# Attention steps placed between the q, k and v layers of a two-block transformer kernel, with the low parts of these layers' weights on VectorE

## The chip, the cores and the metric

The kernel runs on one core of a Trainium2 chip. The metric is device time in microseconds (us), the median of the timed runs. TensorE (PE) multiplies, VectorE (DVE) and ScalarE (ACT) work element by element, GpSimd (POOL) does too, SyncE (SP) starts transfers. Every engine works through a queue of its own in order and meets the others at semaphores.

## What is computed

Two transformer blocks in a row on 256 tokens of width 1024, float32. The first is a mixer (gated delta rule and an S5 state-space layer), a cross attention `xa` (4 heads of 256) and a gated feed-forward layer. The second has two layers: stick-breaking and MoBA attention with rotary positions (`ab`), then forgetting attention (`fox`), each followed by a memory cross attention (`xa0`, `xa1`, 4 heads of 64) and a feed-forward layer with a short convolution. Cut to what the change touches:

```python
def sb_moba_mixer(h, positions, w_in, w_out):
    qkv = h @ w_in                                   # q, k, v: 16 heads of 64
    o_sb = stick_breaking_attention(q[:, :8], k[:, :8], v[:, :8])
    o_moba = moba_attention(rope(q[:, 8:], positions), rope(k[:, 8:], positions), v[:, 8:])
    return merge_heads(jnp.concatenate([o_sb, o_moba], axis=1)) @ w_out
def fox_mixer(h, w_in, b_f, w_out):
    q, k, v, f_logit = ...                           # from h @ w_in; 16 heads of 64
    log_f = jax.nn.log_sigmoid(f_logit + b_f)
    return merge_heads(forgetting_attention(q, k, v, log_f)) @ w_out
# stick breaking, per head: z = q k^T / 8
#   log_1mb = where(past, log_sigmoid(z) - z, 0); tail = reverse cumsum(log_1mb) - log_1mb
#   a = where(past, exp(log_sigmoid(z) + tail), 0); o = a v
# forgetting, per head: p = softmax(q k^T / 8 + c[t] - c[s], causal); c = cumsum(log_f)
```

With 256 tokens a MoBA block holds them all, so that attention is a plain causal softmax.

## The kernel before

Activations lie feature-major: 8 tiles of 128 features x 256 tokens. All weights come in one list of slots of 128 x 1024 float32 (512 KB), transferred in turn into six `w_raw` buffers. From `x_v` on a slot is split: ACT writes the high part `w_hi` (line 857), DVE (line 1303) or POOL (line 1945) the rest `w_lo`, each into one of three buffers. `lo_on_pool` says which: outside the feed-forward layers every third slot is POOL's. `three` (line 351) then makes each product of three fp32r products: high x high, low input, low weight. `ahead(s)` stands in the ACT and DVE queues and makes the parts up to slot s+2; a high part waits until PE has left the slot three before.

A feature-major layer (`fm`) takes one slot of 8 blocks for one output tile, 24 products of 256 columns. A token-major one (`tok_slot`, the v layers) takes two input tiles per slot, 12 products of 512 columns. Accumulators are banks 0 and 1 in turn; a product waits until the one two before is read out. Reading out multiplies with `R`, the reciprocal root mean square (`scaled`, line 1438), which is computed while the first products of a layer run. Its sums are `mean_square` (line 423), f32 products; a f32 product is two passes in the trace. In front of `ab` two such norms follow each other (`fin1`, `mx0`).

The order is written out by hand on each engine: all of `ab_q`, `ab_k` (with `rope` products, line 778, in between), `ab_v`, then the attention head by head, then `ab_o`; `fox` alike. In `attention` a head's scores (line 684; for fox selector products 690 and 692 and the mask 694) go to one bank, DVE takes the maximum (1671, 1672 or 1674), ACT the exponentials (1163), DVE divides (1680, 1683), PE turns the probabilities (707), ACT copies them (1173 to 1176), PE multiplies with v (`values`, 727), ACT and DVE split the result (1186, 1697). Three heads are in flight. Stick breaking has scores (803, 804), three ACT steps, two DVE steps (1820, 1822), cumulative sums as products (814 to 816), and a DVE step (1813). A head has 64 features, so its products use half of PE's rows (scores) or columns (values). During these attentions the slots of the next layer wait, as all buffers are full.

Of the kernel before, what the change touches and what calls it, by code (L numbers as in the profile page):

```python
# [8 lines left out]

# [7 lines left out]
P = 128  # L17
T = 256
D = 1024
KD = D // P  # L20
# [6 lines left out]
NF = 22  # L27
# [16 lines left out]
FIRST, _n = {}, 0  # L44
for _name, _kind, _k, _m in LINEARS:
    FIRST[_name] = _n
    _n += 3 * NF if _kind == "ffn" else _k * _m // 8
SLOTS = _n
SHAPE = {name: (k, m) for name, _, k, m in LINEARS}
# [19 lines left out]
MEM_SUMS_AT = {6 + m: m for m in range(KD)}  # L69

# [98 lines left out]
def lo_on_pool(s):  # L169
# [3 lines left out]
    for name in ("ffn0", "ffn1", "ffn2"):  # L173
        if FIRST[name] <= s < FIRST[name] + 3 * NF:
            return (s - FIRST[name]) % 3 == 2
    return s % 3 == 0


def build(nc, io, known):
    with ExitStack() as ctx:  # L180
# [53 lines left out]
        def scores_bank(h):  # L234

            return bank[(2, 3, 0, 1)[h % 4]]

        def tok_bank(name, nh, tt):


            if nh and name != "x_v":
                return bank[6 + tt]
            return bank[(ACC_OF[name] + 2 * nh + tt) % 2]
# [35 lines left out]
        PROB = area(6144, 2, 2, T)  # L279
        PROBT = area(7168, 2, 2, T)  # L280
        SBA, SBM = area(8192, 3, 384), area(9344, 2, 384)
# [15 lines left out]
        def _(sp):  # L297
            sp.dma_start(PARS[:], io["pars"]).then_inc(*inc("pars_landed", "pars", by=16))
            sp.dma_start(H[:], io["x"]).then_inc(*inc("x_landed", "x", by=16))
            for s in range(SLOTS):  # L300
# [16 lines left out]
                sp.dma_start(RAW[:, s % RAW_SLOTS, :], io_w[s]).then_inc(  # L317
# [9 lines left out]
        def _(pe):  # L327
            mm, tp = nc.tensor.matmul, nc.tensor.transpose
            acc = [0]

            def acc_take(n=1):

                t0 = acc[0]
                acc[0] += n
                for t in range(t0, t0 + n):
                    if t >= 2:
                        pe.wait_ge(*at(("acc", t - 2)))
                return t0
# [25 lines left out]
            def fm(name, m, x, x_ready, sums=None, whole_sum=None):  # L364
# [3 lines left out]
                t = acc_take()  # L368
                out = bank[t % 2][:, 0:T]
                order = [(k + 4) % 8 for k in range(8)] if name == "w_out" else range(K)  # L370
                for n, k in enumerate(order):
                    b = m * K + k
                    s = FIRST[name] + b // 8
# [16 lines left out]
            def tok_slot(name, j, x, x_ready):  # L390
# [3 lines left out]
                s = FIRST[name] + j  # L394
                slot_ready(s)
                for b in range(8 * j // w, 8 * (j + 1) // w):
                    nh, k = b // K, b % K
                    if k == 0 and (nh == 0 or name == "x_v"):
                        acc_take(2)
                    if nh == 0:  # L400
                        pe.wait_ge(*at(x_ready(k)))
                    for tt in range(TT):
                        out = tok_bank(name, nh, tt)[:, 0:w * P]
# [10 lines left out]

            def tok(name, x, x_ready):
                for j in range(SHAPE[name][0] * SHAPE[name][1] // 8):
                    tok_slot(name, j, x, x_ready)
# [159 lines left out]
            for s, (name, j) in enumerate(STEPS):  # L577
# [8 lines left out]
                if s == 0:  # L586
                    pe.wait_ge(*at("cons"))
                    fm(name, j, x, lambda k: ("whole", ready, k), lambda k: mean_square("x", k))
# [1561 lines left out]
```

## Time and profile before

| | |
|---|---|
| timed runs, us | 1395.13, 1417.39, 1421.9 (median 1417.39) |
| profiled execution, us | 1396.11, of which 1394.3 is the span that the profile shows |
| mean granted PE clock | 0.953 |
| busy, us | PE 1301.1, DVE 843.1, ACT 685.9, POOL 257.7 |
| transferred | 187.90 MB, 135 GB/s over the span |

Times in the profile count from the start of the span. The profiled execution is one run; stage and step times of it add up to its own 1396.11 us and not to the median. PE, DVE and ACT overlap, so their sums exceed the span.

### The profile page before, as it was taken

What the parts mean: (1) busy time and instruction counts of PE and PEld (TensorE: products, weight loads), DVE (VectorE), ACT (ScalarE), POOL (GpSimd) and SP (SyncE); (2) the same over time, 40 slices, a digit from 0 to 9 for tenths busy, and PEclk for the clock granted to TensorE, in tenths of its full rate; (3) what the DMA queues carried; (4) which work ended last, traced back from release to release, by engine and by line L of the source; (5) the groups of instructions that cost most, each with busy time, mean ns of one, the idle gap of its engine ahead of it and who ended that gap; (6) DMA issues with size and microseconds to landing.
All of it is one profiled execution on the core that took longest, in us unless ns stands there. A gap on an engine that the chain in (4) does not pass through costs nothing.

```text
span 1394.3 us, 22964 instructions
## 1 busy us (share of the span) xinstructions
PE 1301.1 (93%) x9136; PEld 1180.3 (85%) x9136; DVE 843.1 (60%) x1511; ACT 685.9 (49%) x1197; POOL 257.7 (18%) x160
## 2 busy tenths in 40 slices
PE   6999899899999999898899799999999996999997
PEld 5777689798999999797648599999997584999996
DVE  2899676564654444565435567777644465677775
ACT  3352525454544444634435455555634455655554
POOL 5000000121222222222002022222222010222221
PEclk9999999989999999999659799999999999999999
DMA  7233322233455555344003145555454032355551
GB/s 308 91 106 108 120 91 91 76 122 121 139 190 185 185 183 184 111 160 166 0 1 125 57 139 188 185 185 183 155 184 161 1 107 76 135 184 181 182 182 46
DMA packets 51225, 187.90 MB, mean 135 GB/s; under 512 B 5680, under 2 KB 5808, under 8 KB 50736
## 3 DMA queue, kind: packets, MB, share of 16 engines
q1 hardware_dynamic: 51120, 186.44, 38.8%
q8 instruction: 73, 1.20, 0.3%
q14 instruction: 32, 0.26, 0.1%
HBM read 185.37 MB, written 1.05 MB: 134 GB/s over the span
## 4 chain that ended last, share of the span: by engine, by line
PE 79%; DVE 8%; ACT 7%; issue 4%; POOL 2%; DMA 0%; DVEq 0%; ACTq 0%; POOLq 0%
PE banks L351 58%; PE banks L727 4%; PE banks L381 4%; PE banks L684 3%; ACT w_hi L857 2%; PE banks L707 2%; PE banks L423 1%; DVE w_lo L1303 1%; PE banks L406 1%; PE banks L545 1%; DVE h L1653 1%; ACT arena L1163 1%; PE banks L474 1%; PE banks L555 1%; DVE a_lo L1315 1%
## 5 line engine op out<-in xcount | busy, mean ns | idle before, releaser
L1945 POOL TENSOR_TENSOR w_lo<-w_raw,w_hi 128x1024 fp32r<-128x1024 f32 x99 | 238.7, 2411 | 1110.4 <-ACT w_hi L857 1110.4
L857 ACT ACTIVATE w_hi<-w_raw 128x1024 fp32r<-128x1024 f32 x313 | 329.0, 1052 | 197.2 <-PE banks L351 190.5
L351 PE MATMUL banks<-a_hi,w_hi 128*128 128x256 f32 x1432 | 413.9, 289 | 7.4 <-DVE arena L1438 4.9
L351 PE MATMUL banks<-a_lo,w_hi 128*128 128x256 f32 x1432 | 407.5, 285 | 0.0
L351 PE MATMUL banks<-a_hi,w_lo 128*128 128x256 f32 x1432 | 407.3, 284 | 0.0
L1303 DVE TENSOR_TENSOR w_lo<-w_raw,w_hi 128x1024 fp32r<-128x1024 f32 x214 | 263.4, 1231 | 90.8 <-ACT w_hi L857 90.7
L351 PEld LDWEIGHTS banks<-a_hi,w_hi 128*128 128x128 f32 x1432 | 277.0, 193 | 10.1 <-DVE arena L1438 5.1
L351 PEld LDWEIGHTS banks<-a_lo,w_hi 128*128 128x128 f32 x1432 | 277.1, 193 | 0.6
L351 PEld LDWEIGHTS banks<-a_hi,w_lo 128*128 128x128 f32 x1432 | 276.8, 193 | 0.0
L351 PE MATMUL banks<-b_hi,w_hi 128*128 128x256 f32 x880 | 257.1, 292 | 18.4 <-DVE h L1653 6.4
L351 PE MATMUL banks<-b_lo,w_hi 128*128 128x256 f32 x880 | 253.3, 288 | 0.0
L351 PE MATMUL banks<-b_hi,w_lo 128*128 128x256 f32 x880 | 253.1, 288 | 0.0
L351 PEld LDWEIGHTS banks<-b_hi,w_hi 128*128 128x128 f32 x880 | 173.1, 197 | 24.5 <-issue 13.8
L351 PEld LDWEIGHTS banks<-b_lo,w_hi 128*128 128x128 f32 x880 | 173.5, 197 | 0.0
L351 PEld LDWEIGHTS banks<-b_hi,w_lo 128*128 128x128 f32 x880 | 173.2, 197 | 0.0
L1206 ACT ACTIVATE arena<-arena,pars 128x256 f32<-128x256 f32 x88 | 53.0, 602 | 131.5 <-DVE arena L1726 131.5
L1726 DVE TENSOR_TENSOR arena<-banks,rstd 128x256 f32<-128x256 f32 x132 | 55.8, 424 | 101.3 <-PE banks L351 93.0
L1732 DVE SCALAR_TENSOR_TENSOR arena<-arena,pars 128x255 f32<-128x255 f32 x88 | 59.8, 680 | 60.7 <-ACT arena L1206 60.7
L381 PE MATMUL banks<-early,w_raw 128*128 128x256 f32 x400 | 94.2, 390 | 0.2 <-ACT v_mem L951 0.2
L381 PEld LDWEIGHTS banks<-early,w_raw 128*128 128x128 f32 x400 | 77.5, 196 | 14.7 <-issue 3.1
L882 ACT ACTIVATE a_hi<-h,pars 128x256 fp32r<-128x256 f32 x64 | 32.4, 506 | 62.4 <-DVE h L1653 60.2
L1163 ACT ACTIVATE arena<-banks,small 128x128 f32<-128x128 f32 (+1 forms) x72 | 30.9, 435 | 61.9 <-PE banks L707 45.3
(324 smaller groups left out, 1531.0 us busy)
## 6 DMA issues: line engine op xcount, KB each, us to landing
w_raw<-in_weights SPq DMA_DIRECT2D x342, 512.0 KB, 3.5
h<-in_x SPq DMA_DIRECT2D x1, 1024.0 KB, 4.9
arena<-in_mem SPq DMA_DIRECT2D x1, 1024.0 KB, 13.2
early<-in_mem SPq DMA_DIRECT2D x1, 1024.0 KB, 14.9
out_h<-h SPq DMA_DIRECT2D x2, 512.0 KB, 2.7
cons<-in_cons SPq DMA_DIRECT2D x1, 962.0 KB, 7.7
arena<-in_late SPq DMA_DIRECT2D x1, 448.0 KB, 4.3
pars<-in_pars SPq DMA_DIRECT2D x1, 290.5 KB, 2.9
```

The lines of the kernel that those rows point to most:

```text
L351: ins = mm(out, l, r, start=start and n == 0, stop=stop and n == 2, skip_group_check=check)
L381: ins = mm(out, raw(s, b % 8), x[:, k, :], start=n == 0, stop=n == K - 1)
L684: ins = mm(out, q[rows, tile, tt * P:(tt + 1) * P], k[rows, tile, 0:keys], start=n == 0, stop=n == len(parts) - 1 and not causal and not bias)
L727: ins = mm(out, v[:, kt, c:c + min(dims, P)], probs(h, kt)[:, lo_t:T], start=kt == 0, stop=kt == TT - 1)
L857: do(WHI[:, n % SPLIT_SLOTS, :], RAW[:, n % RAW_SLOTS, :], ACT.Copy).then_inc(*inc("w_hi_made", ("w_hi", n)))
L882: do(x[0][:, m, :], src, ACT.Copy, scale=par(g, m)).then_inc(*inc("input_hi", ("a_hi", tag, m)))
L1163: do(PROB[:, h % 2, tt, 0:keys], scores_bank(h)[:, tt * T:tt * T + keys], ACT.Exp, bias=SMALL[:, o + tt:o + tt + 1], accum_out=SMALL[:, o ...
L1206: do(FC[:, 2 * (f % 2) + g, :], FS[:, 2 * (f % 3) + g, :], ACT.Identity, scale=par(f"cw{conv}", 88 + g * NF + f), bias=par(f"cb{conv}", g ...
L1303: v.tensor_tensor(WLO[:, n % SPLIT_SLOTS, :], RAW[:, n % RAW_SLOTS, :], WHI[:, n % SPLIT_SLOTS, :].bitcast(F32), ALU.subtract).then_inc(*i ...
L1726: v.tensor_tensor(x, acc_bank(t), R[:], ALU.mult).then_inc(*inc("ffn_scaled", ("fs", tag, f, g), ("acc", t)))
L1732: step(v.scalar_tensor_tensor(c[:, 1:T], x[:, 0:T - 1], par(f"cw{conv}", 44 + g * NF + f), c[:, 1:T], ALU.mult, ALU.add), label="ffn_conv")
L1945: g.tensor_tensor(WLO[:, n % SPLIT_SLOTS, :], RAW[:, n % RAW_SLOTS, :], WHI[:, n % SPLIT_SLOTS, :].bitcast(F32), ALU.subtract).then_inc(*i ...
```

## The change

The slots of `ab` and `fox` come in another order: four v slots (half of v), for fox the gate's slot, then 20 units u: q 0, k 0, q 1, k 1, ... q 7, k 7 and the other four v slots. All sixteen heads are treated as eight pairs p, two heads in the two halves of a 128-row tile. Tables such as `SB_SCORES_AT` say after which unit PE issues which step of which pair; DVE and ACT follow one and two units later. A pair's products alternate between its two heads and go to two banks (scores) or to two halves of one (values); DVE and ACT steps take both heads at once. Both masks of a head become one product. The values of pairs 4 to 7 are issued after the first four products of `ab_o` (`fox_o`). `xa` is woven into `x_q` in the same way, head by head. `xa0` and `xa1` stay whole, but issue all scores first. The cosine and sine steps (`rope_args`, `rope_angles`) move into `ffn0`. `lo_on_pool` is false for all slots of the `ab` and `fox` q, k, v and gate layers. The first accumulators of a stage lie in banks 0, 1, 6 and 7. The last quarter of v is read out by DVE.

```diff
+def unit(b, u):
+
+    return (f"{b}_{'qk'[u % 2]}", u // 2) if u < 16 else (f"{b}_v", u - 12)
+
+
+def in_turn():
+    for name, kind, k, m in LINEARS:
+        if name in ("ab_q", "fox_q"):
+            b = name[:-2]
+            yield from ((f"{b}_v", j) for j in range(4))
+            if b == "fox":
+                yield "fox_f", 0
+            yield from (unit(b, u) for u in range(20))
+        elif name[:3] in ("ab_", "fox") and name[-2:] != "_o":
+            continue
+        else:
+            yield from ((name, j) for j in range(3 * NF if kind == "ffn" else k * m // 8))
+
+
+SLOT = {x: s for s, x in enumerate(in_turn())}
+ROW_OF = [ROW[name] + j for name, j in SLOT]
...
+SB_SCORES_AT = {2 * p + 2: p for p in range(4)}
+SB_CUM_AT = {2 * p + 4: p for p in range(4)}
+SB_VALUES_AT = {2 * p + 5: p for p in range(4)}
+ROPE_Q_AT = {2 * p + 1: p for p in range(4, 8)}
+ROPE_K_AT = {2 * p + 2: p for p in range(4, 8)}
+MOBA_SCORES_AT = {2 * p + 3: p for p in range(4, 8)}
+MOBA_TURN_AT = {2 * p + 5: p for p in range(4, 8)}
+FOX_SCORES_AT = {2 * p + 2: p for p in range(8)}
+FOX_TURN_AT = {2 * p + 4: p for p in range(8)}
+FOX_VALUES_AT = {2 * p + 5: p for p in range(4)}
+NEXT_V = {"mx0": "ab_v", "mx1": "fox_v"}
+X_SCORES_AT = {2: 0, 4: 1, 6: 2}
+X_TURN_AT = {4: 0, 6: 1}
+X_VALUES_AT = {5: 0, 7: 1}
...
+    for name in ("ab", "fox"):
+        if FIRST[f"{name}_v"] <= s < FIRST[f"{name}_o"]:
+            return False
...
+            for u in range(KD):
+                fm("x_q", u, A, lambda k: ("a_lo", "xa", k), whole_sum="xa")
+                if u in X_SCORES_AT:
+                    x_scores(X_SCORES_AT[u])
+                if u in X_TURN_AT:
+                    x_turn(X_TURN_AT[u])
+                if u in X_VALUES_AT:
+                    x_values(X_VALUES_AT[u])
+            x_scores(3)
+            x_turn(2)
+            x_values(2)
+            x_turn(3)
+            residual("x_o", B, lambda k: ("att_in", "xa", k), ahead_of={6: lambda: x_values(3)})
...
+            def pair_values(block_, p, ready, probs):
+
+                pe.wait_ge(*at(ready))
+                if p >= 4:
+                    for tt in range(TT):
+                        pe.wait_ge(*at((f"{block_}_v", "out", 1, tt)))
+                else:
+                    pe.wait_ge(*at((f"{block_}_v", "out", 0, 1)))
+                if p == 0:
+                    pe.wait_ge(*at(("acc", LAST_IN_6[block_])))
+                elif p <= 4:
+                    pe.wait_ge(*at(("o_free", block_, p - 1)))
+                else:
+                    pe.wait_ge(*at(("pt", "fox" if block_ == "fox" else "moba", 6 if p < 7 else 7)))
+                o = values_bank(p)
+                for kt in range(TT):
+                    for e in range(2):
+                        ins = mm(o[HALF[e], kt * P:T], VF[:, kt, (2 * p + e) * 64:(2 * p + e) * 64 + 64],
+                                 probs[:, e, 0:T] if kt == 0 else probs[:, e, T:384], start=kt == 0, stop=kt == 1)
+                ins.then_inc(*inc("values_done", ("o", block_, p)))
...
+            def mask(b):
+
+                blocks_0_2 = bank[b].rearrange("p (a b) -> p a b", a=4)[:, 0:3:2, :]
+                return mm(blocks_0_2, BFC[:, 0, :], BFC[:, 1, :].unsqueeze(1).to_broadcast([P, 2, P]),
+                          start=False, stop=True, skip_group_check=True)
+
+            def pair_scores(p):
+
+                for tt in range(TT):
+                    for e, b in enumerate(pair_banks(p)):
+                        mm(bank[b][:, tt * P:tt * P + (tt + 1) * P], QF[HALF[e], p, tt * P:(tt + 1) * P],
+                           KF[HALF[e], p, 0:(tt + 1) * P], start=tt == 0, stop=False, skip_group_check=True)
...
+            for j in range(4):
+                tok_slot("ab_v", j, A, lambda k: ("a_lo", "mx0", k), sums_mx0)
+            for u in range(20):
+                name, m = unit("ab", u)
+                if u < 16:
+                    fm(name, m, A, lambda k: ("a_lo", "mx0", k))
+                else:
+                    tok_slot(name, m, A, lambda k: ("a_lo", "mx0", k))
+                if u == 1:
+                    rstd_cols("mx0", R)
+                if u in ROPE_Q_AT:
+                    rope("ab_q", ROPE_Q_AT[u])
+                if u in ROPE_K_AT:
+                    rope("ab_k", ROPE_K_AT[u])
+                if u in SB_SCORES_AT:
+                    sb_scores(SB_SCORES_AT[u])
+                if u in MOBA_SCORES_AT:
+                    moba_scores(MOBA_SCORES_AT[u])
+                if u in SB_CUM_AT:
+                    sb_cum(SB_CUM_AT[u])
+                if u in MOBA_TURN_AT:
+                    pair_turn("moba", MOBA_TURN_AT[u])
+                if u in SB_VALUES_AT:
+                    p = SB_VALUES_AT[u]
+                    pair_values("ab", p, ("sb_a", p), SBA[p % 2])
...
+            def memory_attention(l):
+
+                tag = f"xa{l}"
+                for p in range(2):
+                    pe.wait_ge(*at((f"m_q{l}", "scaled", p)))
+                    pe.wait_ge(*at((f"m_k{l}", "scaled", p)))
+                    for tt in range(TT):
+                        for e, b in enumerate(pair_banks(p)):
+                            ins = mm(bank[b][:, tt * T:(tt + 1) * T], QF[HALF[e], p, tt * P:(tt + 1) * P],
+                                     KM[HALF[e], l, p, :], start=tt == 0, stop=True, skip_group_check=True)
+                            if tt == 1:
+                                ins.then_inc(*inc("scores_done", ("s", tag, 2 * p + e)))
+                for h in range(4):
+                    pe.wait_ge(*at(("p", tag, h)))
+                    for tt in range(TT):
+                        for kt in range(TT):
+                            ins = tp(bank[2 + h][:, kt * T + tt * P:kt * T + tt * P + P],
+                                     MPROB[h // 2][:, h % 2, tt, kt * P:(kt + 1) * P], ident)
+                    ins.then_inc(*inc("turned_done", ("tp", tag, h)))
+                    if h >= 2:
+                        memory_values(l, h - 2)
+                for h in range(2, 4):
+                    memory_values(l, h)
...
+            for u in range(1, 20):
+                if u <= 16:
+                    q_or_k("ab", u - 1)
+                if u == 1:
+                    dve.wait_ge(*at("late"))
+                if u == 2:
+                    cols("mx0", 0)
+                if u - 1 in ROPE_Q_AT:
+                    rope("ab_q", ROPE_Q_AT[u - 1])
+                if u - 1 in ROPE_K_AT:
+                    rope("ab_k", ROPE_K_AT[u - 1])
+                if u - 1 in SB_CUM_AT:
+                    sb_arg(SB_CUM_AT[u - 1])
+                if u - 2 in SB_SCORES_AT:
+                    sb_keep_past(SB_SCORES_AT[u - 2])
+                if u - 2 in MOBA_SCORES_AT:
+                    pair_norm("moba", MOBA_SCORES_AT[u - 2])
+                if u - 1 in MOBA_SCORES_AT:
+                    pair_max("moba", MOBA_SCORES_AT[u - 1])
+                ahead(SLOT[unit("ab", u)])
+                if u - 1 in SB_VALUES_AT:
+                    pair_lo("ab", SB_VALUES_AT[u - 1])
```

How this moves the instructions shows at two places. The first is PE in stage ab. Before, the moba heads stand behind all layers; the rows are one head and a piece of the next (707 turns, 684 scores, 694 mask, 727 values):

```order
3190 L684 MATMUL banks<-arena 128x128
3191 L694 MATMUL banks<-bf_consts 128x128
3192 L684 MATMUL banks<-arena 128x256
3193 L694 MATMUL banks<-bf_consts 128x128
3194 L727 MATMUL banks<-arena 64x256
3195 L727 MATMUL banks<-arena 64x128
3196 L707 MATMUL banks<-cons,arena 128x128 x3
3197 L684 MATMUL banks<-arena 128x128
3198 L694 MATMUL banks<-bf_consts 128x128
```

After, unit 11 (`ab_k` 5): the last product of its slot (line 398), then the rope product of q 5 (879), scores of pair 4 (840), masks (833), values of pair 3 (826), then the next slot:

```order
3010 L398 MATMUL banks<-a_hi,w_lo 128x256
3011 L879 MATMUL banks<-arena 128x256
3012 L840 MATMUL banks<-arena 128x128 x2
3013 L840 MATMUL banks<-arena 128x256 x2
3014 L833 MATMUL banks<-bf_consts 128x2x128 x2
3015 L826 MATMUL banks<-arena 64x256 x2
3016 L826 MATMUL banks<-arena 64x128 x2
3017 L398 MATMUL banks<-a_hi,w_hi 128x256
```

The same products now stand between two slots, in twos, and the turns come two units later.

The second is DVE in stage ab. Before, around k 5 of `ab_k` (1438 reads out a tile, 1789 to 1791 are rope, 1303 a low part):

```order
494 L1438 SCALAR_TENSOR_TENSOR arena<-banks,rstd 128x256
495 L1789 TENSOR_TENSOR arena<-banks,arena 128x256
496 L1790 TENSOR_TENSOR arena<-arena 128x256
497 L1791 TENSOR_TENSOR arena<-arena 128x256
498 L1438 SCALAR_TENSOR_TENSOR arena<-banks,rstd 128x256
499 L1789 TENSOR_TENSOR arena<-banks,arena 128x256
500 L1790 TENSOR_TENSOR arena<-arena 128x256
501 L1791 TENSOR_TENSOR arena<-arena 128x256
502 L1303 TENSOR_TENSOR w_lo<-w_raw,w_hi 128x1024
```

After, unit 13 and the start of unit 14 (1678 reads out, 2092 to 2094 rope, 1952 and 1955 divide, 1546 a low part, 1944 and 1945 maxima):

```order
547 L1678 SCALAR_TENSOR_TENSOR arena<-banks,rstd 128x256
548 L2092 TENSOR_TENSOR arena<-banks,arena 128x256
549 L2093 TENSOR_TENSOR arena<-arena 128x256
550 L2094 TENSOR_TENSOR arena<-arena 128x256
551 L1952 RECIPROCAL small<-small 128x4
552 L1955 TENSOR_TENSOR arena<-arena,small 128x2x128
553 L1955 TENSOR_TENSOR arena<-arena,small 128x2x256
554 L1546 TENSOR_TENSOR w_lo<-w_raw,w_hi 128x1024
555 L1678 SCALAR_TENSOR_TENSOR arena<-banks,rstd 128x256
556 L2092 TENSOR_TENSOR arena<-banks,arena 128x256
557 L2093 TENSOR_TENSOR arena<-arena 128x256
558 L2094 TENSOR_TENSOR arena<-arena 128x256
```

Every unit now has its low part on DVE, and the attention's steps stand in front of it.

## Rows read from the trace of the kernel before

**Rows 1.** The page, part 1: TensorE's busy time, share, instructions.
```profile
PE 1301.1 (93%) x9136; PEld 1180.3 (85%) x9136; DVE 843.1 (60%) x1511; ACT 685.9 (49%) x1197; POOL 257.7 (18%) x160
```

**Rows 2.** Table by stage (start:end, us, busy of PE, PEld, DVE, ACT, POOL; clock; DMA).
```profile
332.00:352.00 20.00, 16.80 (x82) 13.83 (x83) 7.69 (x19) 7.74 (x24) 0.00 (x0) 1.00 0.09 28
...
658.00:734.00 76.00, 65.60 (x217) 40.53 (x217) 25.57 (x71) 32.82 (x90) 0.45 (x1) 0.61 0.02 8
767.00:788.00 21.00, 14.88 (x50) 8.03 (x51) 6.54 (x19) 7.13 (x24) 0.00 (x0) 0.67 0.11 41
996.00:1073.00 77.00, 75.34 (x526) 70.27 (x525) 37.86 (x61) 36.48 (x49) 19.29 (x8) 1.00 0.49 168
1073.00:1125.00 52.00, 48.16 (x275) 28.39 (x276) 22.39 (x87) 26.13 (x107) 0.00 (x0) 1.00 0.05 17
```

**Rows 3.** Chain that ended last: start us, us, what.
```profile
389.39 175.90 PE banks L351 x1464
...
569.28 0.58 PE banks L351 x3
...
579.10 1.28 ACT L862
...
586.96 26.02 PE banks L351 x192
...
649.37 7.53 PE banks L351 x33
...
734.05 9.97 PE banks L351 x72
...
1124.63 5.96 PE banks L351 x48
```

**Rows 4.** Timeline of PE, one head of the fox attention (start, us).
```profile
1081.13 0.86 PE L727 MATMUL banks<-arena 128*64 128x256 f32 x4
1081.92 0.55 PE L707 MATMUL banks<-cons,arena 128*128 128x128 f32 x3
1082.40 0.49 PE L684 MATMUL banks<-arena 64*128 64x128 f32 x2
...
1083.09 0.70 PE L684 MATMUL banks<-arena 64*128 64x256 f32 x2
1083.72 0.28 PE L690 MATMUL banks<-fox_selector,arena 96*128 96x256 bf16 x1
...
1084.10 0.65 PE L727 MATMUL banks<-arena 128*64 128x256 f32 x2
```

**Rows 5.** The chain in the S5 stage: full passes, row groups, column groups.
```profile
107.34 7.11 PE banks L381 x32
114.45 1.06 PE banks L459 x8
...
119.16 1.85 PE banks L474 x16
```

**Rows 6.** Groups by line and shape, DVE, 634 to 734 us (busy, mean ns).
```profile
L1303 DVE TENSOR_TENSOR w_lo<-w_raw,w_hi 128x1024 fp32r<-128x1024 f32 x5 | 6.1, 1222 | 1.4 <-ACT w_hi L857 1.4
...
L1820 DVE SCALAR_TENSOR_TENSOR arena<-banks,arena 128x384 f32<-128x384 f32 x8 | 4.4, 552 | 6.1 <-ACT arena L1262 6.1
...
L1789 DVE TENSOR_TENSOR arena<-banks,arena 128x256 f32<-128x256 f32 x4 | 1.7, 425 | 3.9 <-PE banks L778 3.1 <-DVE h L1804 0.7
L1680 DVE RECIPROCAL small<-small 128x2 f32<-128x2 f32 x8 | 1.2, 156 | 2.0 <-ACT arena L1163 2.0
```

**Rows 7.** Timelines of DVE and of POOL, 647 to 651 us.
```profile
647.60 2.62 DVE L1804 SCALAR_TENSOR_TENSOR h<-h,pars,mem_rstd 128x256 f32<-128x256 f32 x1
...
647.50 2.44 POOL L1945 TENSOR_TENSOR w_lo<-w_raw,w_hi 128x1024 fp32r<-128x1024 f32 x1 [7.24 <-ACT w_hi L857]
```

**Rows 8.** Timeline of PE, memory attention xa1, and what follows it.
```profile
1157.09 1.99 PE L684 MATMUL banks<-k_mem,arena 64*128 64x256 f32 x12 [0.69 <-DVE arena L1438]
...
1173.61 0.39 PE L351 MATMUL banks<-b_hi,w_hi 128*128 128x256 f32 x1
```

More of the change, by code:

```diff
@@ L10 @@
+import itertools
 from contextlib import ExitStack
@@ new lines, in rope @@
+            def rope(name, p):
+                pe.wait_ge(*at((name, "scaled", p)))
+                if name == "ab_q" and p == 4:
+                    pe.wait_ge(*at("late"))
+                    pe.wait_ge(*at(("acc", LAST_IN_7["ab"])))
+                else:
+                    pe.wait_ge(*at(("rope_read", *(("ab_q", p) if name == "ab_k" else ("ab_k", p - 1)))))
+                mm(bank[7][:, 0:T], rot_m, (QF if name == "ab_q" else KF)[:, p, :], start=True,
+                   stop=True).then_inc(*inc("rope_done", ("rope", name, p)))
@@ L1266, in _ @@
+            tok_out("ab_v", 1, VF, 0, (0,))
+            pair_turned("moba", 7)
+            for p in range(4, 8):
+                pair_hi("ab", p)
             residual("ab_o", "xa0", "g2_xa0")
             plain("m_q0")
-            attention("xa0", 4, 64, False)
+            memory_attention("xa0")
             residual("m_o0", "f1", "g2_ffn0")
             ffn("ffn1", "f1", "mx1", "g2_mix1", conv=0)
-            plain("fox_q")
-            plain("fox_k")
-            plain("fox_f")
-            for s in range(2):
-                ahead(FIRST["fox_v"] + s)
+            ahead(SLOT["fox_f", 0])
@@ L1277, in _ @@
+            ahead(SLOT[unit("fox", 0)])
             act.wait_ge(*at("fox_x"))
@@ L1826, in _, with rope @@
-            attention("moba", 8, 64, True, 4)
+            dve.wait_ge(*at("mx0_second"))
+            step(v.tensor_tensor(R, MR1, MR2, ALU.mult), ("r", "mx0"))
+            ahead(SLOT[unit("ab", 0)])
+            def rope(name, p):
+                x = (QF if name == "ab_q" else KF)[:, p, :]
+                dve.wait_ge(*at(("rope", name, p)))
+                if name == "ab_q" and p == 4:
+                    dve.wait_ge(*at("cos"))
+                else:
+                    dve.wait_ge(*at(("roped", *(("ab_q", p) if name == "ab_k" else ("ab_k", p - 1)))))
+                step(v.tensor_tensor(POSF, bank[7][:, 0:T], SIN, ALU.mult), ("rope_read", name, p), label="rope_vec")
+                step(v.tensor_tensor(x, x, COS, ALU.mult), label="rope_vec")
+                v.tensor_tensor(x, x, POSF, ALU.add).then_inc(*inc("rope_vec", ("roped", name, p)))
@@ L1827, in _ @@
+            v_out("ab")
+            for p in range(4, 8):
+                pair_lo("ab", p)
             residual("ab_o", "xa0", "g2_xa0")
             plain("m_q0", QF, "xa0", 0.125)
[L1829 removed]
+            memory_attention("xa0")
             residual("m_o0", "f1", "g2_ffn0")
             ffn("ffn1", "f1", "mx1", "g2_mix1", conv=0)
[L1832 to L1834 removed]
+            ahead(SLOT["fox_v", 3])
@@ L1841, in _ @@
+            ahead(SLOT[unit("fox", 0)])
+            q_or_k("fox", 0)
+            ahead(SLOT[unit("fox", 1)])
             dve.wait_ge(*at("fox_ln"))
```

831 lines of the change are left out of this document (458 added, 373 removed).

## The prediction

> **What bounds the kernel now.** I read the page first, then the table by stage, then the chain of waits. TensorE (PE) is busy 93% of the span [rows 1], so time can only go where PE runs slowly or does work that can be had for less. The table by stage [rows 2] shows where that is. From 658 to 734 us (the stick-breaking and moba attentions) PE is busy 65.6 of 76 us, but its granted clock is 0.61 and the DMA queues move 8 GB/s: PE waits, computes at half clock and no weight moves. The fox attention (1073 to 1125) runs at full clock, PE busy 48.2 of 52. In the layers in front of it (996 to 1073) PE is busy 75.3 of 77 us while VectorE (DVE) works 37.9 and ScalarE (ACT) 36.5: both are half idle there and have room for attention work. The chain [rows 3] gives the unit prices: a slot of a feature-major layer (24 products) costs 175.90/1464 x 24 = 2.88 us of PE, a slot of a token-major one (12 products with 512 columns) 7.53/33 x 12 = 2.74 us.
>
> **Stage ab, PE's work at full clock.** The new order begins with the first four slots of `ab_v`. Each of its eight input tiles costs six products of 0.228 us and two mean-square sums, f32, two passes of 0.22 us each: 2.25 us, so 18.0 us. PE starts them when the old kernel starts `ab_q` (569.3) [rows 3]. In the old kernel PE stands until 587.0, because the accumulator of `ab_q` 0 can only be emptied once `R` exists. Now `ab_v` fills banks 0 and 1 without `R`, and q 0 and k 0 have banks of their own, so 5.8 us of products cover the chain that makes `R` (I estimate 4 to 5 us from the last sum: eight steps on ACT and DVE of the 0.43 us kind of [rows 6], and a table load of 1.28 [rows 3]). The rest: 16 q and k slots, 46.1 us; four more v slots, 11.0; eight rope products of 0.44, 3.5.
>
> The attention itself goes by pairs of heads, and a pair's products alternate between halves of the array. The trace of before has such alternation elsewhere [rows 5]: a full f32 pass of 256 columns takes 7.11/32 = 0.222 us; eight passes that alternate between row groups take 1.06 us, 0.133 each; sixteen that alternate between column groups take 1.85 us, 0.116 each. The memory attention's first three heads, which happen to follow each other in opposite halves, need 1.99 us for 12 passes, 0.166 each [rows 8]. I take the first two. Scores of a pair (four passes with 256 columns, four with 128): 4 x 0.133 + 4 x 0.067 = 0.80 us. Values: 0.46 + 0.23 = 0.70. Without overlap either is 1.33. The single head of now pays more [rows 4]: its 256-column score product stands 0.63 us before the next starts, its values 0.79, its three turns 0.48, the whole head 2.97 from one values step to the next. A stick-breaking pair: 0.80 + cumulative products 2 x 512 columns at full size, 1.78, + 0.70 = 3.3; four are 13.1. A moba pair: 0.80 + two masks 0.25 + turns 0.96 + 0.70 = 2.7; four are 10.8. For the entry into each of 28 inserted pieces I add 0.15 us, the surplus of a half-array product over the full one (0.63 against 0.44) [rows 4, 5], rounded down: 4.2. Sum 18.0 + 46.1 + 11.0 + 3.5 + 13.1 + 10.8 + 4.2 = 106.7. `ab_o` would begin at 569.3 + 106.7 = 676.0 instead of 734.1 [rows 3], with the values of pairs 4 to 7 counted though they now lie behind its first four products. **58 us less.** Half of that is the clock: the 76 us at 0.61 are 46 at full clock. The rest is pairing, waits of PE and the covered `R`.
>
> TensorEngine Tiling (Array Packing) of the Trainium skill, section Theoretical Speedup, allows up to 2x where a dimension is 64 or less; by it scores and values of a pair would cost 0.67 each instead of 0.80 and 0.70, 2.6 us less over 16 pairs. The same page, Key Properties, says that a change of tiling mode drains the engine, which speaks against products of other shapes woven in; the trace agrees in that the lone product above costs 0.63.
>
> **Who else must keep up in ab.** PE reaches unit u+2 two units after DVE may begin its low part, so a late DVE queue stops PE. DVE rows [rows 6]: low part 1.22, scaled output and each rope step 0.43, 384 columns 0.55 (768: 0.95), reciprocal 0.16. Heaviest are units 9 to 17, where rope, moba and the end of stick-breaking meet. DVE has there 9 low parts 11.0, 8 scaled 3.4, 8 ropes 10.3, four 768-column steps 3.8, three maxima (0.42 + 0.69) 3.3, three normalisations (0.16 + 0.42 + 0.69) 3.8, two low parts of values 0.8: 36.4 us. PE has eight q/k and v units, rope, three and a half moba pairs and two values, in all 40 us. So DVE is 90% full and PE stays the bound. Eight of the stage's 24 low parts were POOL's. Taking them from POOL costs DVE 9.8 us, hidden as just counted, and gives some back: in 647.6 a step with two SBUF inputs took 2.62 us instead of under 0.5, as long as POOL's own low part ran [rows 7]. The GPSIMD Engine Reference of the Trainium skill, section Specifications, says that the two share their SBUF interface when a DVE instruction has two SBUF inputs; the trace agrees, 2.62 us.
>
> ACT has per two units 2 x 1.06 of high parts and four exponentials, some 6 us against 9. `ahead` for a later slot stands in front of the attention steps in its queue and waits only for a slot that PE has left. The cosine and sine steps move into `ffn0`, where DVE has half its time free and PE is 5.8 us behind the prepared slots: 2.6 us hidden. Weights: a slot's transfer needs 3.1 us at the 168 GB/s of the layers [rows 2] and units now last 3.3 to 5.4 us, so transfers are easier than before.
>
> **Stage fox.** From 996: 8 x (1.37 + 0.44) = 14.5; `fox_f` 2.9; q, k 46.1; v 11.0; eight pairs of 0.80 + selector and mask products 1.0 (0.38 and 0.27 per head, less half of the masks) [rows 4] + 0.96 + 0.70 = 3.46, 27.7; 20 pieces x 0.15 = 3.0. Sum 105.2, `fox_o` at 1101.2 instead of 1124.6 [rows 3]: **23 us less**. A two-unit period is 9.3 us for PE and about 6 for DVE.
>
> **Memory attentions xa0, xa1.** Now some 20 us (at clock 0.67) and 16.5 us from the first scores to the first product of `m_o` [rows 2, 8]. With all scores issued first, DVE carries it: 1.1 us to the first head's scores, four maxima of 0.69, four normalisations of 0.85, then turn 0.6, copy 0.6, values 0.6, high and low 0.8: 9.7 to the second tile, about 9.6 to the first product. **10 and 7 us less.** Stage xa (332 to 352) has full-size products that cannot be paired; PE is busy 16.8 of 20 us [rows 2], and scores, turn and values of its last head are still exposed. I take 2 us, with bounds 0 and 3.
>
> **Sum.** 58 + 23 + 17 + 2 = 100 us. The profiled execution took 1396.1 us (span 1394.3), so it would be 1296. The three timed runs were 1395, 1417 and 1422: the median lies 21 above the profiled one. Part of that may be half-clock time that goes with this stage; I add some 9 and forecast **1305 us**. A measurement of this kernel can hardly tell less than 2% (28 us) from no change.
>
> **Rivals.**
> *Halves do not overlap in this place* (other banks, weight loads of 64 rows between passes). For it: the three heads above reach only 0.166 [rows 8]. Against it: both alternations in rows 5. Price 16 pairs x (0.53 + 0.63) = 19 us: 1324.
> *DVE's queue becomes the bound.* In-order waits (cumulative sum, logarithm, maximum) stand in front of each low part; 90% leaves little, and 768-column broadcasts have no row. If each of 36 woven units ends 0.7 us late, 25 us: 1330. The weave would then do only part of what it says, since PE would stand at the weights instead of at the scores.
> *The clock falls in the woven stage* as it did from 672 on, after PE had stood for scores. At 0.61 the 107 us of ab would last 68 longer: 1373. Against it: the fox attention with the same kinds of products held 1.00 [rows 2].
> *Slower:* each inserted piece waits for its answer from ACT and DVE, unhidden, with the layers' products stopped behind it. A round trip per head is 16.5/4 = 4.1 us [rows 8]; 55 pieces would cost 226 against the 100 saved. It decides from 1.8 us per piece on; at 4.1 the kernel takes 1530. Against it: one to two units (2.9 to 5.8 us) lie between a piece and its answer.
>
> **How the numbers follow.** Forecast 0.58, no overlap 0.12, DVE 0.16, clock 0.07, slower 0.04, other 0.03. The range runs from 1280 (pairs at 0.67, no entry cost, median as the fastest runs) to 1345 (both middle rivals together, or one of them with the 21 us); clock and slower are left out. Faster by over 2%: the first three and part of the clock case, 0.89. Within 2%: rest of clock and other, 0.07. Slower: 0.04.
>
> **What would show it.** Right: `ab_o` some 107 us after `ab_v`'s first product; granted clock 1.0 in between; a pair's eight score passes in 0.8 us; fox stage 105 us; memory attentions under 10.5. Wrong: PE waiting for `w_lo` from DVE for more than 5 us in all, or for probabilities; score pairs of 1.3 us; clock under 0.9 in the woven stages; transfers of weights landing late.

## Result and profile after

The changed kernel takes 1316.33 us (median of 1313.02, 1316.21, 1316.45 and 1318.37), the kernel before 1406.26 in the runs beside it (1394.44 to 1421.9): a ratio of 0.9435, interval 0.9402 to 0.9469. The forecast was 1305, range 1280 to 1345. The runs of before fall into two groups, near 1395 and near 1419; those of after do not, and the ratio compares with the lower group. The profiled execution took 1313.02 us with a span of 1311.2, so 83.1 us of span were saved where 100 were forecast.

The page of after, part 1, answers to [rows 1]:

```profile
PE 1226.5 (94%) x9112; PEld 1140.2 (87%) x9112; DVE 849.1 (65%) x1445; ACT 668.4 (51%) x1136; POOL 219.7 (17%) x144
```

PE is busy 74.6 us less with nearly the same number of instructions: fewer of them run at half clock, and heads no longer run singly. The mean clock is 0.984 instead of 0.953.

The table by stage of after, with the columns of [rows 2]: passage into `ab_v`, woven ab, `ab_o`, xa0, passage into `fox_v`, the rest of fox.

```profile
562.70:598.00 35.30, 23.88 (x82) 18.51 (x83) 9.80 (x17) 14.25 (x26) 0.00 (x0) 0.85 0.17 56
598.00:681.30 83.30, 83.30 (x628) 74.55 (x628) 64.52 (x109) 48.31 (x83) 2.12 (x1) 1.00 0.39 127
681.30:717.60 36.30, 34.20 (x283) 31.93 (x281) 23.25 (x38) 20.42 (x34) 8.01 (x4) 1.00 0.44 142
717.60:728.20 10.60, 8.08 (x41) 4.54 (x41) 6.02 (x13) 6.66 (x22) 0.00 (x0) 0.84 0.18 63
936.20:958.90 22.70, 17.00 (x68) 13.14 (x67) 9.88 (x16) 10.23 (x17) 0.00 (x0) 0.92 0.33 113
958.90:1045.00 86.10, 84.50 (x684) 75.97 (x684) 52.65 (x95) 46.48 (x105) 2.38 (x1) 1.00 0.37 122
```

The second row is the change at work: 83.3 us without one moment in which PE stands, at full clock, with weights at 127 GB/s. The stage of before that had clock 0.61 and 8 GB/s [rows 2] is gone. The first and the fifth row are new: while PE works on the first four v slots it is busy 23.9 of 35.3 us and 17.0 of 22.7, and the clock sinks.

Stage by stage, from first product to first product in both chains, where the time went:

| part | before | after | saved | forecast |
|---|---|---|---|---|
| start to `x_q` | 311.2 | 306.9 | 4.2 | 0 |
| `x_q` to ffn0 | 78.2 | 75.8 | 2.4 | 2 |
| ab's first product to `ab_o` | 164.8 | 118.6 | | |
| `ab_o` to xa0 | 33.6 | 36.3 | 43.5 for both | 58 |
| xa0's scores to `m_o` | 19.9 | 10.6 | 9.4 | 10 |
| fox's first product to `fox_o` | 128.3 | 108.8 | | |
| `fox_o` to xa1 | 32.5 | 35.2 | 16.8 for both | 23 |
| xa1's scores to `m_o` | 16.5 | 10.3 | 6.2 | 7 |

The 2.7 us more in the `_o` layers are the values of four pairs that the change put there. The 4.2 us at the start are no work of the change: there the two traces differ in granted clock only (0.83 in before's 40 to 60 us, 1.00 in after's). That part of the kernel is the same in every experiment below, and its clock changes from run to run: 0.83 in the profiled runs of experiments 4 and 6, 0.91 in those of experiments 1 and 2, 1.00 in that of experiment 5. So these 4.2 us are chance.

The chain of after between 566 and 582 us shows the new stand, that is, the time in which PE waits with work left to do:

```profile
566.56 0.45 PE banks L470 x2
...
567.10 0.39 ACT squares L1044
...
567.94 1.05 ACT w_hi L1029
...
569.01 0.04 DVE w_lo L1546
569.05 1.11 issue
570.16 0.42 DVE h L2052
...
570.61 0.49 DVE a_lo L1558
...
571.24 2.31 PE banks L398 x6
573.54 1.71 PE banks L470 x4
```

Read it as a ring. PE forms the sums of tile 1 (L470); that frees the buffer for the squares of tile 2; behind them in ACT's queue stands the high part of the next v slot; DVE's low part waits for it, and behind that low part stand `h` of tile 3 and `a_lo` of tile 2, on which PE waits. PE stands 3.81 us, and what follows runs at half clock: four sums in 1.71 instead of 0.86 us. The same comes again at 577 and 587. In front of fox the ring closes three times too, with stands of 1.90 us; behind the first two PE goes on at full clock, and only behind the third (953.4) does half clock follow.

The woven part in the chain of after, for [rows 4]:

```profile
607.02 0.63 PE banks L852 x4
607.66 0.22 PE banks L855 x4
...
648.33 0.86 PE banks L840 x8
649.19 0.33 PE banks L833 x2
649.51 0.80 PE banks L826 x8
650.32 3.06 PE banks L398 x24
...
653.81 2.87 PE banks L398 x24
...
658.29 0.66 PE banks L806 x6
```

Scores of a pair take 0.86 us (0.85 in stick breaking), masks 0.33, values 0.80, the turns 0.66, and the slot behind values 3.06 instead of 2.87.

The chain in xa1, for [rows 8]:

```profile
1080.16 1.11 PE banks L935 x8
...
1083.25 0.69 DVE arena L1921
...
1088.45 1.89 PE banks L957 x12
```

`m_o` begins at 1090.48, 10.3 us after the first scores, and VectorE's maxima and divisions fill the middle of it, as counted.

### The profile page after: what moved, and what is told of

It reads as the page before. It is cut to its first block, busy times and chain, and to the rows that moved or that the text cites. A ratio compares the mean times of both kernels' runs of the same rounds, so it can differ in the third digit from the quotient of the medians.

```text
span 1311.2 us, 22739 instructions
## 1 busy us (share of the span) xinstructions
PE 1226.5 (94%) x9112; PEld 1140.2 (87%) x9112; DVE 849.1 (65%) x1445; ACT 668.4 (51%) x1136; POOL 219.7 (17%) x144
## 4 chain that ended last, share of the span: by engine, by line
PE 81%; DVE 9%; ACT 5%; issue 4%; DMA 1%; POOL 1%; SPq 0%; DVEq 0%; ACTq 0%
PE banks L398 62%; PE banks L429 5%; ACT w_hi L1029 2%; PE banks L470 2%; DVE w_lo L1546 1%; PE banks L455 1%; PE banks L592 1%; PE banks L826 1%; DVE h L1889 1%; DVE a_lo L1558 1%; PE banks L521 1%; PE banks L602 1%; PE banks L840 1%; ACT squares L1044 1%; PE banks L608 1%
## 5 line engine op out<-in xcount | busy, mean ns | idle before, releaser
L2279 POOL TENSOR_TENSOR w_lo<-w_raw,w_hi 128x1024 fp32r<-128x1024 f32 x83 | 200.7, 2418 | 1065.5 <-ACT w_hi L1029 1065.5
L1546 DVE TENSOR_TENSOR w_lo<-w_raw,w_hi 128x1024 fp32r<-128x1024 f32 x230 | 283.6, 1233 | 101.1 <-ACT w_hi L1029 100.8
L398 PE MATMUL banks<-b_hi,w_hi 128*128 128x256 f32 x880 | 254.3, 289 | 21.7 <-DVE h L1889 7.1
L398 PEld LDWEIGHTS banks<-b_hi,w_hi 128*128 128x128 f32 x880 | 170.4, 194 | 28.2 <-issue 14.9
L398 PEld LDWEIGHTS banks<-b_lo,w_hi 128*128 128x128 f32 x880 | 170.7, 194 | 0.0
L1054 ACT ACTIVATE a_hi<-h,pars 128x256 fp32r<-128x256 f32 x64 | 32.5, 507 | 70.4 <-DVE h L1889 57.2
L470 PE MATMUL banks<-squares,cons 128*128 128x256 f32 x112 | 35.6, 434 | 13.5 <-DMA cons<-in_cons 9.9
```

Source lines behind the costliest of these rows:

```text
L398: ins = mm(out, l, r, start=start and n == 0, stop=stop and n == 2, skip_group_check=check)
L470: ins = mm(bank[2][:, 0:T] if out is None else out, con("ones_d", P), SQ[:, sq_slot(tag, m), :], start=m == 0 and tag != "mem1", stop=m == ...
L1054: do(x[0][:, m, :], src, ACT.Copy, scale=par(g, m)).then_inc(*inc("input_hi", ("a_hi", tag, m)))
L1546: v.tensor_tensor(WLO[:, n % SPLIT_SLOTS, :], RAW[:, n % RAW_SLOTS, :], WHI[:, n % SPLIT_SLOTS, :].bitcast(F32), ALU.subtract).then_inc(*i ...
L2279: g.tensor_tensor(WLO[:, n % SPLIT_SLOTS, :], RAW[:, n % RAW_SLOTS, :], WHI[:, n % SPLIT_SLOTS, :].bitcast(F32), ALU.subtract).then_inc(*i ...
```

## Experiments

The times are medians of the timed runs; where a stage is named it is read from the profile of that kernel.

**1. The high part in front of the squares.**

```diff
                         hi_gained(tag_next, m, A, H[:, m, :], g_next, ("h", tag_next, m))
+                    if tag_next in NEXT_V and m in (1, 3, 5):
+                        ahead(SLOT[NEXT_V[tag_next], m // 2])
...
-                    if tag_next in NEXT_V and m in (2, 4, 6):
-                        ahead(SLOT[NEXT_V[tag_next], m // 2 - 1])
```

> The changed kernel, but in the passage from a feed-forward layer to the v slots ScalarE makes the high part of the next v slot after the a_hi of tiles 1, 3, 5, in front of the squares, instead of behind the squares of tiles 2, 4, 6. Theory (queue ring): PE stands three times 3.8 us in front of ab and three times 1.9 us in front of fox because sum k, squares, high part (1.05), low part (1.23), h, a_lo follow one another before the next tile; the half clock that follows each stand costs some 1.7 us more. Then the first four v slots of ab fall from 35.3 to 19 to 23 us and those of fox from 22.7 to 16 to 18, in all 17 to 22 us, and the kernel takes 1294 to 1300. Rival (two squares buffers): the pace is set by sum to squares to sum, whatever stands behind; then under 4 us change, 1312 or more. Rival (clock alone): the stands stay, only their order changes, and the four slots stay above 30.

Measured: 1293.08 us, ratio 0.9264 (0.9246 to 0.9281), a span of 1291.3. The table by stage (passage, woven ab, passage of fox):

```profile
565.47:583.70 18.23, 18.23 (x82) 15.27 (x83) 9.56 (x17) 13.64 (x26) 0.00 (x0) 1.00 0.32 109
583.70:667.28 83.58, 83.43 (x628) 74.61 (x628) 64.77 (x109) 48.57 (x83) 2.15 (x1) 1.00 0.38 127
922.56:937.29 14.73, 14.73 (x68) 12.15 (x67) 9.91 (x16) 10.73 (x18) 0.00 (x0) 1.00 0.42 140
```

The passages fall to 18.2 and 14.7 us with no stand at all, 25 us less, and a little below what I had expected (19 to 23 and 16 to 18); woven ab is as it was. The ring is shown, both rivals fall, and this version is faster than both kernels.

**2. The low part later in VectorE's queue.**

```diff
-                    if tag_next in NEXT_V and m in (2, 4, 6):
+                    if tag_next in NEXT_V and m in (3, 5, 7):
```

(in VectorE's loop; ScalarE's is that of after)

> The changed kernel; ScalarE's queue as it is, but VectorE makes the low part of the next v slot after h of tiles 3, 5, 7 instead of 2, 4, 6, so that a_lo of tiles 2, 4, 6 stands in front of it. Theory (the ring of queues, counted link by link): the ring from a sum to the next a_lo stays 3.8 to 4.2 us long, but PE now has one more tile's work inside it, 2.25 us in front of ab and 1.83 in front of fox. The three stands in front of ab shrink from 3.8 to about 1.9, those in front of fox from 1.9 to nearly nothing: the four v slots take 26 to 31 us (35.3 before) and 15 to 18 (22.7), 12 to 18 us less in all, 1298 to 1306. Rival (only the high part's place behind the squares counts): 1312 or more.

Measured: 1297.61 us. The two passages:

```profile
568.28:591.26 22.98, 19.01 (x82) 15.06 (x83) 10.04 (x17) 14.79 (x27) 0.00 (x0) 1.00 0.27 89
930.30:945.32 15.02, 15.02 (x68) 12.10 (x67) 9.82 (x16) 10.26 (x18) 0.00 (x0) 1.00 0.41 136
```

Better than I had counted: the stands in front of ab shrink to at most 1.5 us each, 4.0 in all (22.98 - 19.01), and behind these no half clock follows, so 23.0 us instead of 26 to 31. Either queue alone, mended at the right link, is enough in front of fox; in front of ab VectorE's leaves these 4.0 us, and ScalarE's nothing.

**3. Low parts back on GpSimd.**

```diff
-    for name in ("ab", "fox"):
-        if FIRST[f"{name}_v"] <= s < FIRST[f"{name}_o"]:
-            return False
```

> The changed kernel, with every third low part of the ab and fox q, k, v layers back on GpSimd. Theory: in the woven stretch PE never waits (busy 83.3 of 83.3 us) and VectorE is 77% busy, so neither engine's low parts are the bound, and moving eight of them changes less than 3 us: 1314 to 1320. Rival (VectorE's queue was saved by the move from GpSimd): GpSimd's 2.4 us low parts slow VectorE's steps and come late, PE waits for w_lo at every third slot by 0.5 us or more, 13 slots: 7 us or more, 1323 and up. Rival (VectorE near its bound): it gets faster by 5.

Measured: 1316.18 us, no difference. VectorE by line and operation in the woven stretch, 598 to 682 us, of this kernel:

```profile
L1543 DVE TENSOR_TENSOR w_lo<-w_raw,w_hi 128x1024 fp32r<-128x1024 f32 x13 | 15.8, 1217 | 1.2 <-ACT w_hi L1026 1.2
L2140 DVE SCALAR_TENSOR_TENSOR h<-h,pars,mem_rstd 128x256 f32<-128x256 f32 x8 | 7.7, 966 | 0.0
...
L2101 DVE TENSOR_TENSOR arena<-arena 128x768 f32<-128x768 f32 x4 | 5.9, 1486 | 0.1
L2091 DVE TENSOR_TENSOR arena<-arena 128x256 f32<-128x256 f32 x8 | 5.5, 688 | 0.3
L2090 DVE TENSOR_TENSOR arena<-arena 128x256 f32<-128x256 f32 x8 | 5.4, 674 | 0.3
```

and the same groups of after:

```profile
L1546 DVE TENSOR_TENSOR w_lo<-w_raw,w_hi 128x1024 fp32r<-128x1024 f32 x20 | 24.4, 1218 | 6.0 <-ACT w_hi L1029 6.0
...
L2104 DVE TENSOR_TENSOR arena<-arena 128x768 f32<-128x768 f32 x4 | 3.8, 958 | 0.1
L2143 DVE SCALAR_TENSOR_TENSOR h<-h,pars,mem_rstd 128x256 f32<-128x256 f32 x8 | 3.8, 478 | 0.0
...
L2094 DVE TENSOR_TENSOR arena<-arena 128x256 f32<-128x256 f32 x8 | 3.4, 426 | 0.3
L2093 DVE TENSOR_TENSOR arena<-arena 128x256 f32<-128x256 f32 x8 | 3.4, 425 | 0.3
```

GpSimd takes seven low parts, 8.6 us, off VectorE, and the four groups shown with two SBUF inputs grow from 14.4 to 24.5. The growth is five single steps of 2.3 to 3.1 us, each running while a GpSimd low part runs; their neighbours keep their length. One of them, from the timelines of VectorE and GpSimd:

```profile
641.09 3.07 DVE L2101 TENSOR_TENSOR arena<-arena 128x768 f32<-128x768 f32 x1
640.95 2.39 POOL L2276 TENSOR_TENSOR w_lo<-w_raw,w_hi 128x1024 fp32r<-128x1024 f32 x1 [14.00 <-ACT w_hi L1026]
```

VectorE is then busy 67.6 us instead of 64.5, and PE still hardly waits (83.6 busy of 85). So this half of the change neither gains nor costs time that these runs can tell.

**4. The same pairs, not woven.** All pieces of pairs come 18 units later, behind the layers (loops run to 40, with the layers only below 20):

```diff
-SB_SCORES_AT = {2 * p + 2: p for p in range(4)}
+SB_SCORES_AT = {2 * p + 20: p for p in range(4)}
...
-FOX_SCORES_AT = {2 * p + 2: p for p in range(8)}
+FOX_SCORES_AT = {2 * p + 20: p for p in range(8)}
```

> The changed kernel, with all pairs' scores, turns, cumulative products and values of ab and fox shifted by 18 units, behind the layers, with the same pairs, batches and distances between pieces. Theory (weaving hides the round trips): PE then waits for ACT and DVE between pieces. Two pairs are in flight; a softmax pair's round trip is about 5 us, a stick-breaking one's about 8 us, so a pair takes 3 to 4.5 us instead of 2.4 to 3.5 of pure PE time, and half clock comes in: ab 25 to 45 us longer, fox 5 to 20: 1346 to 1380. Rival (pairing was the gain, weaving nearly nothing): under 10 us more, 1326 or less.

Measured: 1378.97 us, 62.6 more than after, near the upper end of my range. Layers and attention of ab in this kernel:

```profile
602.25:663.50 61.25, 61.07 (x452) 57.93 (x451) 44.09 (x72) 24.42 (x27) 1.49 (x1) 1.00 0.53 172
663.50:727.28 63.78, 38.15 (x177) 26.90 (x178) 22.12 (x37) 23.45 (x55) 0.89 (x1) 0.59 0.03 9
```

The same pieces that cost 22 us between the layers (83.3 - 61.3) cost 63.8 behind them, at clock 0.59. With 2.8 for the values that lie in `ab_o` they make 66.6 against the 76 of single heads [rows 2]: pairing is worth 9 us there, together with all that came with it (one product for both masks, steps of DVE and ACT for two heads at once, the last values moved into `ab_o`), which no run takes apart. Weaving is worth 42. In fox weaving is worth 16.7 (108.8 us against 125.5). The layers with the passage take 96.5 us here (from 567.0) and 87.6 before (569.3 to 656.9, [rows 3]): with the ring closed, the layers in the new order take 9 us more than in the old. With it open they should take 8 less; that is an estimate, 96.5 less the 17.1 of experiment 1, and not a run.

**5. Head by head instead of alternating.** Nothing but the nesting of two loops:

```diff
-                for tt in range(TT):
-                    for e, b in enumerate(pair_banks(p)):
+                for e, b in enumerate(pair_banks(p)):
+                    for tt in range(TT):
```

(for stick-breaking scores and for values alike)

> The changed kernel, but scores and values of a pair are issued head by head instead of alternating between the two halves of the array. Theory (alternation makes the passes overlap): a pair's scores go from 0.86 to 1.2 to 1.35 us and its values from 0.80 to 1.2 to 1.35, 16 pairs, so 12 to 16 us more: 1328 to 1333. Rival (what made heads dear was the entry and the wait, not the order): under 4 us more, and the score pair stays under 1.0.

Measured: 1314.45 us, nothing lost; a pair's scores take 0.86 us as before. My theory of the order fell. The timeline shows why. In this kernel the source has, for a stick-breaking pair, 256 columns (852) and 128 columns (854) of the first head, then both of the second. PE began them otherwise:

```profile
613.90 0.71 PE L852 MATMUL banks<-arena 64*128 64x256 f32 x4
614.44 0.39 PE L854 MATMUL banks<-arena 64*128 64x128 f32 x4
```

All four passes of 256 columns, of both heads, start before the first of 128. The second head's half does not wait for the first head's passes in front of it. So the order in the source changed, and the order of execution did not.

**6. Both heads in the same half.**

```diff
-                        mm(bank[b][:, tt * P:tt * P + (tt + 1) * P], QF[HALF[e], p, tt * P:(tt + 1) * P],
-                           KF[HALF[e], p, 0:(tt + 1) * P], start=tt == 0, stop=False, skip_group_check=True)
+                        mm(bank[b][:, tt * P:tt * P + (tt + 1) * P], QF[HALF[0], p, tt * P:(tt + 1) * P],
+                           KF[HALF[0], p, 0:(tt + 1) * P], start=tt == 0, stop=False, skip_group_check=True)
```

> The changed kernel, with the scores of both heads of a pair computed from the first head's q and k (rows 0 to 63), so both use the same half of the array; the odd heads' scores are therefore not computed. Issue head by head instead of alternating changed nothing, so two theories are left. Theory (the halves overlap, whatever the order within a pair): with one half alone nothing can overlap, a pair's eight score passes go from 0.86 to about 1.5 us (4 x 0.22 + 4 x 0.11 + entry), 16 pairs: 10 us more, 1323 to 1328. Rival (a pass of 64 rows costs 0.11 in itself, whichever half): nothing changes, 1314 to 1319.

Measured: 1326.71 us, 10.4 more. The chain:

```profile
611.18 1.06 PE banks L852 x4
612.24 0.45 PE banks L855 x4
...
655.11 1.50 PE banks L840 x8
656.61 0.33 PE banks L833 x2
```

1.50 us instead of 0.86. So the halves do overlap, for scores. What counts is that the two heads lie in different halves and follow each other at once; the passes of the second half run beside those of the first even when all four stand behind them in the source (experiment 5). For values, which use half of the columns, no run takes the overlap away; their 0.69 to 0.80 us against the 1.33 of the prediction speaks for it.

**7 and 8. Half of, or the whole low part a second time.**

```diff
+                        if FIRST["ab_v"] <= n < FIRST["ab_o"] or FIRST["fox_v"] <= n < FIRST["fox_o"]:
+                            step(v.tensor_tensor(WLO[:, n % SPLIT_SLOTS, 0:512], RAW[:, n % RAW_SLOTS, 0:512],
+                                            WHI[:, n % SPLIT_SLOTS, 0:512].bitcast(F32), ALU.subtract))
```

(0:1024 in the second)

> The changed kernel, with half of every low part of the ab and fox q, k, v and gate slots computed a second time on VectorE (0.6 to 0.7 us more per slot). Of the 83.3 us of woven ab VectorE then works 64.5 + 20 x 0.65 = 78, in the busiest stretch (33.96 of 40 now) 40 of 40. Theory (free time on VectorE counts, the queue's order is loose enough): 3 to 10 us slower, most of it in the two passages in front of the v slots, 1319 to 1326. Rival (VectorE's queue is on the edge, each woven unit ends late when a low part does): 0.6 us for each of 36 units, 22 us or more, 1338 and up.

> The changed kernel, with every low part of the ab and fox q, k, v and gate slots computed twice on VectorE (1.3 us more per slot). Work of VectorE in woven ab 64.5 + 20 x 1.3 = 90 us against 83.3 of PE, in fox 52.7 + 21 x 1.3 = 80 against 86. Theory: VectorE is now the bound of ab (10 to 15 us longer with what the unevenness adds), fox loses 2 to 8, the passages 5 to 10: 1335 to 1350. Rival (queue on the edge already): 1.2 us for each of 36 units, 45 us: 1360 and up. If it takes under 1325, VectorE was further from the bound than its busy time says.

Measured: 1327.01 and 1345.93 us, 10.7 and 29.6 more; the first is 1 us above my range, the second inside it. Woven ab with half of it again, and with all:

```profile
602.50:687.40 84.90, 83.66 (x628) 74.64 (x628) 77.10 (x128) 48.24 (x83) 2.17 (x1) 1.00 0.38 125
```

```profile
606.00:698.50 92.50, 86.46 (x628) 75.91 (x628) 86.16 (x128) 47.40 (x83) 2.06 (x1) 0.98 0.35 114
```

VectorE at 77 of 85 us costs the stretch 1.6 us; at 86 of 92.5 it is the bound and costs 9.2. Fox, with the same 13 us more, loses 3.3 at 65 of 89, part of it at its first scores, which wait for VectorE 2.1 us instead of 1.0. Of the 10.7 us of the first kernel 5.8 arise in the two passages, where every low part lies in the ring. So woven ab has room for most of 13 us more of VectorE's work; the rival of the full queue is refuted at the load of after.

**9. Turns one unit after the scores.**

```diff
-FOX_TURN_AT = {2 * p + 4: p for p in range(8)}
+FOX_TURN_AT = {2 * p + 3: p for p in range(8)}
```

> The changed kernel, with the turns of the fox pairs one unit after their scores instead of two. Theory (each piece needs its distance): PE comes to the turns 2.9 us after the scores, the probabilities are ready after some 4.7 (maximum 1.1 and its place in the queue 0.4, exponentials 1.8, division 1.2), so PE stands 1.8 us per pair, eight pairs 14 us, plus half clock behind the stands if it comes: 1328 to 1336. Rival (the answers have long been there): under 3 us, 1319 or less.

Measured: 1328.82 us, 12.5 more. One pair in the chain:

```profile
986.34 2.89 PE banks L398 x24
...
989.25 0.42 DVE arena L1678
989.68 0.10 DVE small L1952
...
989.80 1.04 DVE arena L1955 x2
...
990.88 0.87 PE banks L806 x6
```

PE stands 1.65 us in front of each of eight turns, 13.1 in all. This is the price of one unit of distance, and the mechanism of the rival that ended slower.

**10. GpSimd for the first two slots of each feed-forward layer**, on top of experiment 1:

```diff
-            return (s - FIRST[name]) % 3 == 2
+            return (s - FIRST[name]) % 3 == 2 or s - FIRST[name] < 2
```

> The kernel with the high part in front of the squares (the best so far, 1293), with the low parts of the first two slots of each feed-forward layer on GpSimd as well. These two stand in VectorE's queue inside the passage from m_o, where VectorE works 16 us for the eight tiles and PE stands 7 of 36 us. Theory (the passage behind m_o is bound by VectorE's queue): two low parts of 1.2 us and the 1.0 us wait in front of one leave it, 2 to 3 us per passage, two of them, up to 1 more in front of ffn0: 1286 to 1290. Rival (GpSimd's 2.4 us parts slow VectorE or come late for the first product): no gain, or 1 to 5 us slower, 1292 to 1298.

Measured: 1292.23 us, ratio 0.9261 (0.9246 to 0.9275), the same as experiment 1. From xa0's scores to the last sum behind `m_o` it takes 25.6 us instead of 26.1. Behind xa1 it takes 24.8 instead of 27.4, but there the clock was 0.93 against 0.81; after, with the same low parts as experiment 1, took 25.9 at 0.93. At equal clock that is half a microsecond to one per passage, not 2 to 3.

## Why the prediction was right, and where it was off

The sign and the range held, and the main mechanism did: the attention steps between the layers keep PE busy at full clock, and experiment 4 shows that this is most of the gain. That 1305 came within 11 us of the median of 1316 is in part luck. The profiled run was forecast at 1296 and took 1313, 17 us more; the 9 us added for the median were 3.3, which hides 6 of them, and another 4.2 came from a better clock at the start, which no term had. By its own steps:

- **First four v slots, 18.0 and 14.5 us: mis-sized, more than the whole of the error.** They took 35.3 and 22.7. The work itself was sized rightly: with the ring open it is 18.2 and 14.7. I took the pace of the tiles from a kernel whose loop had no `ahead` in it, and wrote that `ahead` "waits only for a slot that PE has left". It does; but in front of it stood squares that waited for PE's sums, and behind it the `h` and `a_lo` on which PE waited. In ab 3 x 3.8 = 11.4 us are stands and the other 5.7 half clock. "PE waiting for `w_lo` from DVE for more than 5 us in all" was one of the prediction's signs of being wrong; it came in this form, PE waiting for an `a_lo` behind a `w_lo`, and in these passages only.
- **The woven remainder, 88.7 and 90.7 us: 2.6 and 1.8 too high** (83.3 + 2.8 for the last values; 86.1 + 2.8). Turns 0.66 instead of 0.96, entries 0.2 only behind some pieces; against it scores 0.86 for 0.80, masks 0.33 for 0.25, cumulative products 1.94 for 1.78.
- **Halves overlap, 0.80 and 0.70:** measured 0.86 and 0.69 to 0.80. The rival without overlap is refuted for scores by experiment 6, and for values by their time. Alternation in the source, on which the prediction built, was not needed.
- **VectorE, 36.4 of 40 us in units 9 to 17:** measured 34.0 of 40 (633 to 673 us), and PE busy all 40. The rival "VectorE's queue becomes the bound", to which I gave 0.16 and a price of 25 us, does not come up: experiments 7 and 8 show slack at the load of after.
- **Low parts from GpSimd, hidden:** right. VectorE's steps with two SBUF inputs, 2.62 us beside a low part of GpSimd in [rows 7], take 0.48 in after, and that gives back more than the low parts cost.
- **Clock 1.0 in the woven stage:** right. Half clock came where I had not looked, behind the stands of the passages.
- **`R` covered by q 0 and k 0:** right in ab, where PE does not stand between the passage and the first scores. In fox the first scores wait 1.0 us for VectorE. The prediction says of before that "PE stands until 587.0"; its trace has PE busy 12.8 of the 17.7 us from 569.3 on, and standing 4.9 just before 587.0. That is what the cover can save.
- **xa0, xa1, xa: 10, 7, 2:** 9.4, 6.2, 2.4. The steps listed for a memory attention add up to 9.9 us, not 9.7; 10.6 and 10.3 were measured.
- **Median 9 us above the profiled run:** 3.3. The larger offset belonged to before.

The sum of the errors: 17.3 + 8.2 too little for the passages, 4.4 too much for the woven parts, and 4.2 of clock at the start, which no term had: 25.5 - 4.4 - 4.2 = 16.9 of the 100 forecast. What is left, each under 1 us, cancels.

## What to carry to other kernels

When work for a later stage is put into a loop that hands tiles from one engine to another, follow every queue from the consumer back to itself: a step that waits for nothing of this stage still closes a ring if a step in front of it waits for the consumer and a step behind it feeds the consumer. Put such a step directly behind the last thing that the consumer already has. Leave between a woven piece and the one that needs its answer as much other work as the measured round trip; one unit too few cost 1.65 us per pair here. Idle time of an engine counted as room although its queue is in order: 12.6 us more of VectorE's work cost woven ab 1.6 us. It did not count for nothing: in fox 12.8 more cost 3.3 with VectorE at 65 of 89 us.

## What the runs showed of the hardware

Score products of 64 rows in different halves of the array overlap also when each head's passes stand together in the source (0.86 us for eight passes in either order, 1.50 in one half), and the trace then shows the second head's passes starting beside the first's, not behind them. Seven low parts moved to GpSimd made VectorE busier (67.6 us against 64.5), because five steps with two SBUF inputs took 2.3 to 3.1 us beside them. In after each stand of 3.8 us in front of ab had a stretch of half clock behind it, 5.7 us lost behind the three; of the three stands of 1.9 us in front of fox only the last had one; behind the stands of up to 1.5 us of experiment 2 the granted clock stayed at 1.00.
